# Gate projections of a mixer as block products, with weight sums on GpSimd

## What is computed

```
proj = jnp.einsum('bsd,dc->bsc', h, w_in)
z_pool, z_sg, z_conv, q, k, v, f_logit, gate_cols = jnp.split(proj, COL_SPLITS, axis=-1)
...
branch = jnp.einsum('bsnc,ncd->bsnd', ys, w_branch)
gates = jax.nn.sigmoid(gate_cols).reshape(B, S, N_BRANCH, D)
merged = jnp.sum(gates * branch, axis=2)
return jnp.einsum('bsd,de->bse', merged, w_out)
```

## Time and profile before

| | us |
|---|---|
| median of 3 runs | 771.3 (769.61 to 771.3) |
| the profiled execution | 771.32 |
| its span, first to last instruction | 769.5 |
| PE busy | 728.6 (95%) |
| DVE busy | 340.7 (44%) |
| ACT busy | 174.2 (23%) |
| POOL busy | 37.5 (5%) |

### The profile page before, as it was taken

How to read it: one execution, slowest core, us unless ns; L and a number is a source line. 1 busy time by engine, 2 the same in 40 slices (tenths; PEclk the granted TensorE clock), 3 DMA queues, 4 the chain that set the end, 5 groups by cost and what they waited for, 6 DMA issues and landing times.

```text
span 769.5 us, 12432 instructions
## 1 busy us (share of the span) xinstructions
PE 728.6 (95%) x5014; PEld 383.3 (50%) x5014; DVE 340.7 (44%) x811; ACT 174.2 (23%) x349; POOL 37.5 (5%) x30
## 2 busy tenths in 40 slices
PE   4899999899999999999999999999999998899995
PEld 1588888788887444333343433334333342233332
DVE  1108593875568686333335333331333332322334
ACT  3213330200000333222222221221222222212223
POOL 0200001111113100000000000000000000000000
PEclk9999999999999999999999999999999999999998
DMA  9999726768869588999999999999999999999991
GB/s 339 379 349 364 228 97 208 242 231 275 273 225 419 230 351 298 378 419 421 417 377 419 420 420 421 415 419 416 422 421 421 416 418 421 420 421 419 421 388 70
DMA packets 76165, 271.46 MB, mean 353 GB/s; under 512 B 4728, under 2 KB 33536, under 8 KB 53456
## 3 DMA queue, kind: packets, MB, share of 16 engines
q1 hardware_dynamic: 74544, 264.78, 88.0%
q0 software_dynamic: 1264, 5.79, 2.1%
q10 hardware_dynamic: 304, 0.13, 0.1%
HBM read 269.62 MB, written 1.05 MB: 352 GB/s over the span
## 4 chain that ended last, share of the span: by engine, by line
PE 72%; DMA 19%; DVE 3%; SPq 3%; ACT 1%; issue 1%; POOLq 0%; ACTq 0%; DVEq 0%
PE bank L1160 71%; DMA ring<-exp_w_dram 16%; DMA ring<-ada_w_dram 2%; SPq L369 2%; PE bank L1518 1%; SPq L372 1%; DMA reg<-reg 1%; DVE part L794 0%; DVE reg L929 0%; DVE bank L1114 0%; DVE reg L996 0%; PE bank L1249 0%; POOLq L115 0%; ACT L630 0%; ACT h_hT L655 0%
## 5 line engine op out<-in xcount | busy, mean ns | idle before, releaser
L1160 PE MATMUL bank<-ring,h_hT 128*32 128x512 f32 (+2 forms) x2112 | 261.1, 586 | 13.2 <-DMA ring<-exp_w_dram 13.2
L1160 PE MATMUL bank<-h_hT,ring 128*128 128x256 f32 x704 | 156.5, 381 | 1.4 <-ACT h_hT L514 1.4
L1160 PEld LDWEIGHTS bank<-ring,h_hT 128*32 128x32 f32 (+1 forms) x2112 | 80.5, 113 | 153.7 <-issue 132.1
L1160 PEld LDWEIGHTS bank<-h_hT,ring 128*128 128x128 f32 x704 | 134.1, 191 | 21.0 <-ACT h_hT L514 1.7
L1160 PE MATMUL bank<-ring,const_misc 128*32 128x512 f32 x1008 | 116.5, 595 | 0.7
L1114 DVE TENSOR_TENSOR bank<-bank,reg 128x512 f32<-128x512 f32 x64 | 44.4, 694 | 54.6 <-PE bank L1160 54.6
L1118 DVE TENSOR_TENSOR y_part<-bank,y_part 128x512 fp32r<-128x512 f32 x64 | 44.2, 691 | 42.5 <-ACT y_part L681 21.2
L1160 PEld LDWEIGHTS bank<-ring,const_misc 128*32 128x32 f32 x1008 | 30.2, 109 | 62.3 <-issue 57.6
L670 ACT ACTIVATE reg<-bank 128x256 f32<-128x256 f32 x32 | 12.3, 386 | 205.7 <-PE bank L1160 205.7
L1097 DVE TENSOR_TENSOR reg<-reg,bank 128x256 f32<-128x256 f32 x32 | 13.5, 421 | 102.3 <-ACT reg L670 102.3
L1160 PEld LDWEIGHTS bank<-take,h_part 128*128 128x128 f32 x288 | 38.9, 190 | 28.6 <-issue 27.6
(11 more groups left out here) (237 smaller groups left out, 465.9 us busy)
## 6 DMA issues: line engine op xcount, KB each, us to landing
ring<-exp_w_dram SPq DMA_DIRECT2D x171, 1024.0 KB, 14.8
ring<-ada_w_dram SPq DMA_DIRECT2D x24, 1024.0 KB, 12.9
ring<-w_in_dram SPq DMA_DIRECT2D x24, 1024.0 KB, 12.3
ring<-exp_w_dram SPq DMA_DIRECT2D x35, 512.0 KB, 13.7
ring<-w_branch_dram SPq DMA_DIRECT2D x4, 1024.0 KB, 12.8
ring<-w_out_dram SPq DMA_DIRECT2D x4, 1024.0 KB, 8.2
ring<-shared_w_dram SPq DMA_DIRECT2D x2, 1024.0 KB, 14.5
spare<-exp_w_dram SPq DMA_DIRECT2D x2, 1024.0 KB, 14.5
```

The costliest lines, as they stand in the source:

```text
L1160: return pe.matmul(o, lhsT, rhs, start=start, stop=stop, skip_group_check=True)
```

## The change

Each branch's gate is computed as a 2x2 by 2x2 block product with seven products in place of eight. h is cut into four blocks A (two halves of the tokens, two halves of the inner dimension), the gate weights of the branch into four blocks B of 512x512, which are four gate units of 1 MB. The seven products are

- P1 = A11 B11 and P2 = A12 B21, of blocks as they are, P3 = S4 B22 and P4 = A22 T4, P5 = S1 T1, P6 = S2 T2, P7 = S3 T3,
- with sums of h made once: S1 = A21 + A22, S2 = S1 - A11, S3 = A11 - A21, S4 = A12 - S2,
- and sums of weights made for each branch: T3 = B22 - B12, T1 = B12 - B11, T2 = T3 + B11, T4 = B21 - T2.

A product is 4 matmuls of 128x128 by 128x512, with tokens on the partitions of the result. PE's order in a branch is P1, P2, P7, P5, P6, P3, P4, then four `branch` tiles. P6 adds to P1's bank, P3 to P5's and P4 to P7's. ACT copies P1, P7 and P1+P6 out of their banks; DVE's `combine` makes the four tiles of the gate in five additions (C_11, C_T, C_22, C_12, C_21), ACT takes their sigmoid (`gate_tile`), and `merge` goes by tokens.

POOL makes the sums: four of 128x512 once (`token_sum`), and four of 128x2048 for each branch (`sums_3_1`, `sum_2`, `sum_4`), 16 in all. T3 is written to `x_sb` (now `w_sum`), and T1, T2 and T4 in place into their units of the ring. So x is loaded a second time, on POOL's queue, after the last P7, and `residual_2` waits for it.

The eight `cast` stand between the sums in POOL's program. `merged` now has tokens on its partitions, so PE turns it (`turn_merged`, 8 transposes for each token half, into banks 0 to 3) and ACT copies it back before the output projection. The first `accumulate`, `accumulate(0)`, is moved forward to a place among the spatial gating's work on DVE. The order of the units in the ring is now, for each branch, four gate units, two `ada`, `branch`, two `ada`. Buffers move (`scale_b`, the turned probabilities), with no change in their work.

```diff
+            def token_sum(i, x, y, op, after=0):
+                if after:
+                    pool.wait_ge(S["t_done"], after)
+                pool.tensor_tensor(h_sum[:, i, :, :], x, y, op).then_inc(S["t_done"], 1)
...
+            def sums_3_1(n):
+
+                arrived(n, B12)
+                arrived(n, B22)
+                if n:
+                    pool.wait_ge(S["prod_done"], N_P * (n - 1) + P_7)
+                pool.tensor_tensor(w_sum, b_block(n, B22), b_block(n, B12), ALU.subtract).then_inc(S["t_done"], 1)
+                arrived(n, B11)
+                pool.wait_ge(S["t_done"], N_S + N_T * n + T_3)
+                pool.tensor_tensor(b_block(n, B12), b_block(n, B12), b_block(n, B11), ALU.subtract).then_inc(S["t_done"], 1)
+
+            def sum_2(n):
+                pool.wait_ge(S["prod_done"], N_P * n + P_1)
+                pool.wait_ge(S["t_done"], N_S + N_T * n + T_1)
+                pool.tensor_tensor(b_block(n, B11), w_sum, b_block(n, B11), ALU.add).then_inc(S["t_done"], 1)
+
+            def sum_4(n):
+                pool.wait_ge(S["prod_done"], N_P * n + P_2)
+                pool.wait_ge(S["t_done"], N_S + N_T * n + T_2)
+                pool.tensor_tensor(b_block(n, B21), b_block(n, B21), b_block(n, B11), ALU.subtract).then_inc(S["t_done"], 1)
...
+            sums_3_1(0)
+            sum_2(0)
+            sum_4(0)
+            sums_3_1(1)
             pool.wait_ge(S["sg_y"], 1)
...
-            for m in range(8):
-                cast(m)
+            cast(0)
+            sum_2(1)
+            sum_4(1)
+            cast(1)
+            sums_3_1(2)
...
+            pool.wait_ge(S["prod_done"], N_P * (NB - 1) + P_7)
+            pool.dma_start(x_sb[:, :, :], a["x"][0].rearrange("(b p) d -> p b d", p=P)).then_inc(S["late_in"], 16)
+            cast(6)
+            cast(7)
...
+            combine(0, C_11)
+            combine(0, C_T)
+            conv_taps(CONV_MORE, TAPS)
+            combine(0, C_22)
...
+            for n in range(1, NB):
+                first = [1, 2, 7, 12][n]
+                if n == 3:
+                    cast_out(4)
+                accumulate(first)
+                combine(n, C_11)
+                cast_out([0, 0, 2, 5][n])
+                accumulate(first + 1)
+                accumulate(first + 2)
+                combine(n, C_T)
+                if n == 2:
+                    cast_out(3)
+                accumulate(first + 3)
+                combine(n, C_22)
+                if n == 1:
+                    cast_out(1)
+                if n < 3:
+                    accumulate(first + 4)
+                combine(n, C_12)
+                if n == 3:
+                    cast_out(6)
+                combine(n, C_21)
+                for q in range(4):
+                    merge(n, q)
...
+            def product(b, lhs, rhs, fresh, last):
+
+                rhs = rhs.rearrange("p (k n) -> p k n", k=4)
+                for k in range(4):
+                    ins = mm(bank[b][:, :], lhs[:, k, :], rhs[:, k, :], fresh and k == 0, last and k == 3)
+                ins.then_inc(S["prod_done"], 1)
...
+            def product_6(n):
+                summed(n, T_2)
+                pe.wait_ge(S["a_read"], N_A * n + 1)
+                product(0, h_sum[:, 1, :, :], b_block(n, B11), False, True)
...
+            def product_4(n):
+                summed(n, T_4)
+                pe.wait_ge(S["a_read"], N_A * n + 2)
+                product(3, a_block(1, 1), b_block(n, B21), False, True)
...
+            def turn_merged(tb):
+
+                pe.wait_ge(S["merged_done"], 10 + 2 * tb)
...
+                for k in range(KD):
+                    ins = pe.transpose(bank[2 * tb + k // 4][:, k % 4 * P:(k % 4 + 1) * P], merged[:, tb, k * P:(k + 1) * P], ident)
+                ins.then_inc(S["prod_done"], 1)
```

More of the change, by code:

```diff
@@ L70 @@
 CONV_FIRST = 15
+CONV_MORE = 25
+BLOCK = [(0, 0), (0, 1), (1, 1), (1, 0)]
+B11, B12, B22, B21 = range(4)
+T_3, T_1, T_2, T_4 = 1, 2, 3, 4
+P_1, P_2, P_7, P_5, P_6, P_3, P_4 = 1, 2, 3, 4, 5, 6, 7
+C_11, C_T, C_22, C_12, C_21 = 1, 2, 3, 4, 5
+N_S, N_T, N_P, N_C, N_A = 4, 4, 7, 5, 3
 def unit_plan():
     units = [("ada", i) for i in range(8)] + [("mix", i) for i in range(8)]
-    for g in range(N_GATE):
-        if g % 4 == 3:
-            units.append(("branch", g // 4))
-        units += [("gate", g), ("ada", 8 + g)]
+    for n in range(NB):
+        units += [("gate", 4 * n + b) for b in range(4)]
+        units += [("ada", N_EARLY + 4 * n), ("ada", N_EARLY + 4 * n + 1), ("branch", n)]
+        units += [("ada", N_EARLY + 4 * n + 2), ("ada", N_EARLY + 4 * n + 3)]
     units += [("out", i) for i in range(4)] + [("sw1", 0), ("sw3", 0)]
@@ L364, in _ @@
                     sp.wait_ge(*used_up(BEFORE[u]))
+                    kind, i = BEFORE[u]
+                    if kind == "gate" and i % 4 == B11:
+                        sp.wait_ge(S["t_done"], N_S + N_T * (i // 4) + T_4)
                 src = source(u)
@@ L601, in square_2 @@
+            for tb in range(TB):
+                act.wait_ge(S["prod_done"], N_P * NB + tb + 1)
+                for q in range(2):
+                    act.activation(merged_T[:, tb, 4 * q:4 * q + 4, :], bank[2 * tb + q][:, :].rearrange("p (k t) -> p k t", k=4), ACT.Copy)\
+                       .then_inc(S["mt_read"], 1)
             def square_2(k):
@@ L922, in _ @@
             conv_norm_1()
-            accumulate(0)
+            combine(0, C_12)
+            combine(0, C_21)
             conv_norm_2()
-            accumulate(1)
-            dve.wait_ge(S["conv_rstd"], 1)
+            merge(0, 0)
+            merge(0, 1)
+            dve.wait_ge(S["conv_sig"], 1)
             for j in range(2):
@@ new lines, in b_block, with summed, product_1, product_2 @@
+            def b_block(n, b):
+                return unit(("gate", 4 * n + b))
+            def summed(n, t):
+                pe.wait_ge(S["t_done"], N_S + N_T * n + t)
+            def product_1(n):
+                ready(("gate", 4 * n + B11))
+                pe.wait_ge(*((S["a_read"], N_A * n) if n else (unit_read[0], 4)))
+                product(0, a_block(0, 0), b_block(n, B11), True, True)
+            def product_2(n):
+                ready(("gate", 4 * n + B21))
+                pe.wait_ge(*((S["c_done"], N_C * (n - 1) + C_11) if n else (unit_read[1], 4)))
+                product(1, a_block(0, 1), b_block(n, B21), True, True)
@@ new lines, in product_3, with branch @@
+            def product_3(n):
+                ready(("gate", 4 * n + B22))
+                pe.wait_ge(S["c_done"], N_C * n + C_T)
+                product(2, h_sum[:, 3, :, :], b_block(n, B22), False, True)
+            def product_4(n):
+                summed(n, T_4)
+                pe.wait_ge(S["a_read"], N_A * n + 2)
+                product(3, a_block(1, 1), b_block(n, B21), False, True)
+            def branch(n, q):
+                tb, cb = [(0, 0), (0, 1), (1, 1), (1, 0)][q]
+                if q == 0:
+                    ready(("branch", n))
+                    pe.wait_ge(*[(S["pool_y"], 2), (S["sg_y"], 1), (S["conv_y"], 1), (S["av_y"], 1)][n])
+                if n == 0 and q < 2:
+                    pe.wait_ge(*[(S["av_y"], 1), (S["sg_y"], 1)][q])
+                else:
+                    pe.wait_ge(S["gb_done"], 4 * n + q - 1)
+                w = unit(("branch", n)).rearrange("p (j d) -> p j d", j=2)
+                for j in range(2):
+                    ins = mm(bank[4 + q % 2][:, :], y[:, n, j, tb * P:(tb + 1) * P], w[:, j, cb * 512:(cb + 1) * 512], j == 0, j == 1)
+                ins.then_inc(S["branch_done"], 1)
@@ L1344, in _ @@
+                if n == 0:
                     pe.wait_ge(S["conv_c"], 1)
                     pe.wait_ge(S["pool_y"], 2)
-                    channel_sum(bank[6], sq_c, S["cvar_done"])
-                if g >= LAG:
-                    branch(g - LAG)
-            for g in range(N_GATE - LAG, N_GATE):
-                branch(g)
+                    channel_sum(bank[6], sq_c, S["csum_done"])
+                branch(n, 0)
+                branch(n, 1)
+                branch(n, 2)
+                if n == NB - 1:
+                    turn_merged(0)
```

254 lines of the change are left out of this document (167 added, 87 removed).

## The result

| | before | after |
|---|---|---|
| median | 770.7 us (769.61 to 771.3) | 841.2 us (838.99 to 843.95) |
| ratio, with its 95% interval | 1 | 1.091 (1.089 to 1.094) |
| the profiled execution, its span | 771.32, 769.5 | 839.43, 837.6 |
| PE, DVE, POOL busy | 728.6, 340.7, 37.5 | 734.3, 401.2, 123.8 |

The change costs 70 us; 842 was predicted, between 805 and 880. The span grew by 68.1 us, and PE's output projection starts 68.1 us later (242.47 in the earlier trace rows, 310.6 now): behind the mixer nothing is lost or won.

A forecast was written before the change was run, and what follows sets the result against it. PE was taken to bound the gate stage before; afterwards POOL's chain delays the output projection from 242.47 to 312, 69.5 us, plus 0.9 for turning: 771.32 becomes 841.7, stated as 842 us, range 805 to 880.

The forecast's parts named there:

- The products: PE's gate stage: 28 products replacing 16 gate units, less turning, save 12.3 us, or 16 with its wait and slow clock gone.
- The price of a sum: POOL: one weight sum of 128x2048 takes 4.8 us, scaled from a 128x512 row of 1.27 us.
- The loading: POOL: each change between sum and reduction loads code, 7 us each, ten in the chain, 70 us.
- The port: DVE beside POOL: a sum holds operations with two SBUF inputs for its whole 4.8 us.
- The chain: From branch 0 through POOL's sums, reductions and loadings, cast(0) at 158 to cast(6) at 304, to the output projection at 312.
- the hold up to `spatial`: DVE in branch 0: T3(0) and T1(0) hold taps 9.6 us, four later sums 19.2; `spatial` moves to 130.
- The slow clock: PE behind each wait: about 1 us lost a time, 0 to 4 us in the chain.
- The cheap loading: Rival for POOL: a loading costs at most 3 us but the port is held; 821 us, chance 0.12.
- The free port: Rival for DVE and POOL: sums do not hold the port, loadings cost 7 us; 813 us, chance 0.12.
- Neither: Rival for the gate stage: loadings and holds cost nothing, POOL hides under PE, saving 16 us; 755 us, chance 0.12.

The follow-up runs named there:

- e3: The changed kernel with weight sums cut to 8 columns and the POOL reductions replaced by TENSOR_TENSOR of 128x512; 755.6 us, 0.980 times before.
- e2: The changed kernel with POOL's 16 weight sums cut to 8 of 2048 columns each, reductions kept; 784.2 us, 1.017 times before.
- e1: The changed kernel with each of POOL's eight reductions replaced by a TENSOR_TENSOR of 128x512 on POOL; 817.2 us, 1.060 times before.
- e4: The changed kernel with the eight reductions made by PE matmuls with a ones matrix, copied by ACT, computation complete; 810.1 us, 1.049 times before.
- e7: The changed kernel with each DVE tap waiting for the one just before it, leaving gaps between taps; 855.3 us in one run.
- e5: e4 with the running sum of `accumulate` in a PSUM bank from the second pair of units on; 792.4 us, 1.028 times before.
- e6: e5 with T4(0) and the sums behind it held until the spatial gating's inputs are done, `accumulate(0)` behind branch 0; 798.2 us, 1.035.

## Why the prediction was right

**The products.** Right: 755 was the time with nothing else, e3 measured 755.6.

**The price of a sum.** 4.8 us taken, 4.5 to 5.0 measured in all but T3(0), which DVE held up.

**The loading.** 7 us taken between 1.3 and 11, from an ACT row and a bound; 5.8 to 10.8 measured, mean 7.7, so 7 us more in the chain than the 70. That it comes with each change of kind, which the order alone had told, is shown by e2, where they stay without the sums' work, and by e1 and e4, where they are gone with the reductions. The 7 was a mean between two bounds far apart, so that it lies near 7.7 is luck, and that it goes with the load traffic (6.65 us mean with the DMA engines idle, 9.5 beside loads) was not foreseen. The Trainium skill's GPSIMD Engine Reference, section Architecture, gives about 6 us for the first call after a loading: the shortest gaps here (5.81, 6.07) are near it, and most of the others above.

**The port.** Right in kind and size: an operation that begins with the sum is held to its end and takes 4.9 to 5.0 us (97.91, 107.83, 198.95). Two things were off. The taps were said to be held by T3(0) and T1(0) for 9.6 us; they were not, POOL was (e7). And the text exposed only operations with two SBUF inputs; a TENSOR_SCALAR of 128x2 with one took 3.44 us at 104.27 (0.17 in e3), and two of 128x128 took 4.62 (0.55 in e3) at 79.60. The trace of before had shown it beside a reduction: TENSOR_SCALAR of 128x256 at 142.12, 2.21 us. Other operations with one input passed beside a sum (a BATCH_NORM_STATS2 at 103.59 in 0.43 us, a RECIPROCAL at 107.74 in 0.17), and so did a TENSOR_SCALAR that wrote into a bank (e5). The Trainium skill's page SBUF — State Buffer, section Who interferes with whom, names `tensor_scalar` as able to contend, by its two-port modes; the rows agree.

**The chain.** Its steps against the profile: `spatial` at 130 (123.7), branch 0 done at 154 (147.6), cast(0) at 158 (152.4), cast(6) done at 304 (301.8), the output projection at 312 (310.6). The recorded terms add up to 130.8, not 130. The step that failed is the hold up to `spatial`, 9.6 and 19.2 us. T3(0) and T1(0) held no taps but four TENSOR_SCALAR of the softmax, for 5.9 us (77.12 and 79.60), and the four sums behind them took 15.9 us from DVE (97.91, 104.27, 107.83, 112.76), since a sum takes from DVE only what is left of it when an exposed operation meets it. 106.0 with these, 3.0 for `accumulate(0)` and less 7.0 of waits taken up gives 123.8; measured 123.6. The chain from cast(0) to cast(6) took 149.4 us against 146: sums 47.0 (48), reductions 22.8 (24.5), loadings 77.3 (70), issue 0.9 (0.5), waits 1.4 (3). So the early start (5.6) and the dear loadings (7.3) nearly cancel, and 842 hit 841 more closely than its terms deserve. From there to the output projection 8.8 (8).

**The slow clock.** "About 1 us a wait" was a gate unit behind a wait of 2.5 us. Behind waits of 10 to 16 us PE lost 3.1 us (10.15 for 7.03), 3.0 (6.56 for 3.60) and 3.3 (13.62 for 10.3). Little of it shows in the time, since POOL, not PE, was the chain, in e2 as well.

**The rivals.** The cheap loading (821) is excluded by the gaps. The free port (813) is excluded by the rows above, and its own condition, loadings without held operations, is nearly e2's: that is 784, since the rival kept the sums' own 48 us in POOL's chain, which e2 has not. With the ten sums at 47.0 in place of e2's 4.4 it would be some 827, an estimate: the rival's 813 had the loadings too cheap and cast(0) at 132, which came at 135.7 even with nothing held. Neither (755) is e3.

## What to carry to other kernels

Before work is given to an engine that seems idle, count what it takes from the engine beside it: here a sum on POOL took up to 4.3 us from DVE, nearly twice the 2.28 that DVE needs to make it. Keep instructions of one kind together on POOL, since each change of kind cost 5.8 to 10.8 us, the most beside heavy loads, and put a running operand into PSUM where DVE has to work beside POOL. When a hold is moved in time, look for what is queued behind it at the new place before building it.

## What the runs showed of the hardware that was not expected

- DVE can keep POOL out. 28 taps without a pause let a sum of 4.5 us wait until their end (12.32 us); with gaps between the taps the sum took 4.53 us and the taps 22.81 in place of 11.16. In e2 a sum of 8 columns took 8.28 us in the same place (66.65 to 74.93), 0.20 to 0.71 elsewhere.
- POOL does not keep DVE out in the same way. Three sums 0.2 us or less apart each held one tap, and one passed between every two: 12 taps took 17.45 us in place of 4.84 (e6).
- A loading does not depend on the width of what comes behind it (7.8 us mean with sums of 8 columns, 7.7 with 2048), but its length goes with the load traffic: 5.7 to 7.6 us at a DMA busy share of 0.03 or less, 7.7 to 10.8 at 0.90 or more, in the changed kernel and e2.
- An `accumulate` step with its running sum in a bank costs nothing extra beside a sum, and by itself hardly more than with both in SBUF (0.75 to 0.78 us).
- A TENSOR_SCALAR of 128x2 with one input in SBUF took 3.44 us beside a sum. One of 128x512 took 4.49 us with its output in SBUF (e4), and 0.76 beside the same sum with its output in a bank (e5).
